# A hybrid decoder trunk: the recurrence, its group norm and the self-attention in one block, with small side work at other places of the recurrence

## The reference

```python
proj = h @ w_in[l]
p_r, p_m, p_g = jnp.split(proj, [RWKV_IN, RWKV_IN + MLA_IN], axis=-1)
# RWKV: w_pre = w0 + tanh(wd) @ w_up ; a = sigmoid(a0 + ad @ a_up) ; then, token by token,
state = state * w_t + (state @ a_t) * b_t + v_t * k_t        # 8 heads of 64x64
y = (y - mean) * rsqrt(var + GN_EPS) * ln_g + ln_b           # group norm of each head
y = (y + sum(r * k * r_k) * v) * (sigmoid(gd) @ g_up)
# MLA: q = rms_norm(c_q) @ w_uq, kv = rms_norm(c_kv) @ w_ukv, rope, rms_norm of q and k, causal attention
# gMLP: u * (tril(ws) @ rms_norm(gelu(v)) + b)
```

## Time and profile before

| | us |
|---|---|
| median of 3 runs | 1892.87 (1888.97 to 1893.78) |
| profiled execution, its own time | 1892.21 |
| its span | 1890.5 |
| PE busy | 1764.2 (93%) |
| DVE busy | 613.0 (32%) |
| ACT busy | 387.6 (21%) |
| recurrence block, layer 0 (201.8 to 256.8) | 55.0 |
| attention block, layer 0 (257.3 to 324.8) | 67.5 |

### The profile page before, as it was taken

How to read it: one execution, slowest core, us unless ns; L and a number is a source line. 1 busy time by engine, 2 the same in 40 slices (tenths; PEclk the granted TensorE clock), 3 DMA queues, 4 the chain that set the end, 5 groups by cost and what they waited for, 6 DMA issues and landing times. The chain is left out here.

```text
span 1890.5 us, 26335 instructions
## 1 busy us (share of the span) xinstructions
PE 1764.2 (93%) x11146; PEld 869.5 (46%) x11146; DVE 613.0 (32%) x1163; ACT 387.6 (21%) x745; POOL 182.0 (10%) x223
## 2 busy tenths in 40 slices
PE   8989989999999999998699998999999999999986
PEld 6435755455444443433353467544554444343322
DVE  7247545136311111110233584522461111111102
ACT  3131254054000000000212313522530000000001
POOL 3000101004000000000300000000040000000001
PEclk9999999999999999999899999999999999999997
DMA  9502204234999999999840220153179999999996
GB/s 378 206 1 34 36 10 172 95 134 163 406 429 426 428 427 428 428 427 427 317 198 0 34 35 4 54 222 134 62 284 412 427 427 427 427 429 427 428 428 238
DMA packets 90489, 494.83 MB, mean 262 GB/s; under 512 B 45646, under 2 KB 50510, under 8 KB 62736
## 3 DMA queue, kind: packets, MB, share of 16 engines
q1 hardware_dynamic: 82672, 475.45, 61.6%
q0 software_dynamic: 7632, 17.74, 2.6%
q10 hardware_dynamic: 80, 0.13, 0.0%
HBM read 465.34 MB, written 36.18 MB: 265 GB/s over the span
## 5 line engine op out<-in xcount | busy, mean ns | idle before, releaser
L2175 PE MATMUL bank<-ring,hT 128*64 128x512 f32 x2048 | 465.8, 597 | 37.6 <-DMA ring<-in_we 31.2
L2175 PEld LDWEIGHTS bank<-ring,hT 128*64 128x64 f32 x2048 | 139.6, 137 | 313.3 <-issue 251.0
L1059 PE MATMUL bank<-hT,ring 128*128 128x512 f32 (+1 forms) x576 | 249.9, 593 | 0.0
L2183 PE MATMUL bank<-ring,arena 128*64 128x512 f32 x1040 | 236.7, 597 | 11.4 <-DMA ring<-in_we 9.4
L1059 PEld LDWEIGHTS bank<-hT,ring 128*128 128x128 f32 (+1 forms) x576 | 107.9, 188 | 138.5 <-issue 137.2
L2160 PE MATMUL bank<-shift_in,arena 128*128 128x256 bf16 (+1 forms) x1440 | 160.0, 268 | 0.0
L2160 PEld LDWEIGHTS bank<-shift_in,arena 128*128 128x128 bf16 x1440 | 129.9, 98 | 62.6 <-issue 48.7
L2228 DVE TENSOR_TENSOR hT<-bank,colp 128x512 f32<-128x512 f32 (+1 forms) x68 | 45.3, 668 | 340.0 <-PE bank L2160 328.5
L2564 ACT ACTIVATE arena<-bank 128x256 f32<-128x256 f32 x65 | 24.9, 383 | 605.0 <-PE bank L2146 605.0
L2193 POOL DMA_INDIRECT expert_rows<-arena,row_places x63 | 62.1, 985 | 847.2 <-DVE arena L2705 818.6
L2183 PEld LDWEIGHTS bank<-ring,arena 128*64 128x64 f32 x1040 | 71.0, 136 | 144.0 <-issue 126.5
(11 more groups left out here) (464 smaller groups left out, 1885.6 us busy)
## 6 DMA issues: line engine op xcount, KB each, us to landing
ring<-in_we SPq DMA_DIRECT2D x193, 2048.0 KB, 22.9
ring<-in_w_in SPq DMA_DIRECT2D x6, 2048.0 KB, 19.2
expert_rows<-ring SPq DMA_DIRECT2D x1, 8448.0 KB, 25.8
ring<-in_w_out SPq DMA_DIRECT2D x4, 2048.0 KB, 9.5
ring<-in_wm SPq DMA_DIRECT2D x2, 2048.0 KB, 7.5
ring<-in_w_in SPq DMA_DIRECT2D x2, 1920.0 KB, 16.7
ring<-in_w_in SPq DMA_DIRECT2D x2, 1664.0 KB, 26.9
ring<-in_w_in SPq DMA_DIRECT2D x2, 1152.0 KB, 28.5
```

The source lines that it names most:

```text
L1059: last = nc.tensor.matmul(B[n % 4][0:w, :], ins_units[unit][:, k, u0:u0 + w], hT[:, k, :], start=k == 0, stop=k == KD - 1)
L2175: last = nc.tensor.matmul(bank[CAP * j:CAP * j + CAP, :], x[:, k, :], ahead_w[4 * j + k] if third else up_w(u, j, k), start=k == 0, stop=k ...
L2183: last = nc.tensor.matmul(bank[CAP * half:CAP * half + CAP, :], hid[u][:, m, :], down_w(slot, m, half), start=m == 0, stop=m == HM - 1)
```

## The change

Four things are done.

- **One block.** The streams of recurrence and attention become functions (`recurrent_pe`, `attention_pe` and so on) that one `nc.Block()` calls one after the other on each engine. The block's end and `end_stage()` between them go. Attention's instructions wait for semaphores of the recurrence instead (`s_yc`, `s_o`, `s_tr`, `s_lv`). The projection's semaphores are cleared by SP at the start of `attention_sp`.
- **Side work moved.** The table below has the places. `latent_means` goes from `fill_last(4)` to `fill_last(0)`, before `products(5, 5)`, and `flip(vT, 2, 7)` behind that.
- **Order at attention's start.** `up_q(0)` goes ahead of the centring, `up_q(1)` ahead of `heads_summed`, `gate(0)` ahead of `spread(0)`. SP's loads of `wsm` and `gbb` wait for the last flip of the recurrence only.
- **Low-rank products.** `lora_a` and `lora_decay` become `lora_pair(0)` and `lora_pair(1)`: each makes two products of either kind, in turn.

| side work | before | after |
|---|---|---|
| GELU of `gv` (ACT) | after `flipped("b", 3)` | after `diagonal(0)` |
| GELU of `uT` (ACT) | after `u_kept(6)` | after `ak_v_kept(0)` |
| squares of `gv` (ACT) | before `u_kept(6)` | before `ak_v_kept(1)` |
| both roots (ACT) | before `out_kept(3)` | before `u_kept(5)` |
| copy of the means (DVE) | before `state_kept(5)` | before `state_kept(0)` |
| transpose of the means (PE) | `fill_first(6)` | `fill_first(3)` |
| columns copied (DVE) | before `state_kept(6)` | before `state_kept(3)` |
| sums of `gv` (DVE) | after `w_added(7)` | before `state_kept(3)` |
| gains of `t14`, `cq2` (DVE) | before `state_kept(3)` | before `state_kept(4)` |
| RoPE products (DVE) | before `state_kept(4)` | before `state_kept(5)` |
| both reciprocals (DVE) | block's end | before `state_kept(5)` |
| scaling of `gv` (DVE) | block's end | before `state_kept(6)` |

The diff, without lines that only change their indentation:

```diff
+            def recurrent_pe(eng):
...
+                def latent_means(b):
+                    for i in range(NT):
+                        t, rows = slice(i * P, (i + 1) * P), slice(32 * i, 32 * i + 32)
+                        nc.tensor.matmul(B[b][rows, 0:P], lat_pick[:, 0, :], sq14[:, t], start=True, stop=False)
...
+                    last.then_inc(s_lp, 1)
...
                         elif q == 3:
+                            eng.wait_ge(s_gm, 16)
+                            nc.tensor.transpose(B[6][:, 0:P], lat_rows, ident[:, :]).then_inc(s_lp, 1)
                             eng.wait_ge(s_tc, FLIPS["k", 2])
                             flip(vT, 3, 7)
...
                             products(4, 5)
                             eng.wait_ge(s_wbc, 2)
-                            flip(vT, 2, 7)
+                            eng.wait_ge(s_la, SQUARES)
+                            latent_means(7)
                             eng.wait_ge(s_gm, 10)
                             products(5, 5)
+                            eng.wait_ge(s_lv, MEANS_KEPT)
+                            flip(vT, 2, 7)
...
-            end_stage()
...
+            def attention_sp(eng):
+                clear(late)
+                eng.wait_ge(s_tr, FLIPS["k", 3])
                     eng.dma_start(wsm, wsT_d[lay].rearrange("a p g n -> p (a g) n")).then_inc(s_gw, 16)
...
+            def attention_pool(eng):
+                eng.wait_ge(s_o, NC)
                     eng.memset(gn_rs, 0.0).then_inc(s_gz, 1)
...
+                eng.wait_ge(s_lv, SCALED)
+                up_q(0)
+                eng.wait_ge(s_yc, NC // 2)
                     for c in range(RC):
                         nc.tensor.matmul(B[c][:, :], head_centre[:, :], rT[:, c, :], start=True,
                                          stop=True).then_inc(s_gn1, 1)
-                    up_q(0)
+                up_q(1)
                     eng.wait_ge(s_gn3, RC)
                     heads_summed(B[4], gn_sq).then_inc(s_gn4, 1)
-                    up_q(1)
                     up_q(2)
-                    eng.wait_ge(s_gn5, 1)
-                    spread(0)
                     eng.wait_ge(s_gn2, RC)
                     gate(0)
+                eng.wait_ge(s_gn5, 1)
+                spread(0)
                     up_q(3)
+                eng.wait_ge(s_lv, KEYS_SCALED)
                     up_k(0)
...
-                    for c in range(RC):
-                        eng.wait_ge(s_ap, c + 1)
-                        eng.activation(X4[:, c, :], B[4 + c][:, :], ACT.Tanh, scale=0.5,
...
+                    for z in range(2):
+                        for n in range(2):
+                            c = 2 * z + n
+                            eng.wait_ge(s_ap, c + 1)
+                            eng.activation(X4[:, c, :], B[4 + 2 * n][:, :], ACT.Tanh, scale=0.5,
...
+            with nc.Block() as block:
...
+                @block.tensor
+                def _(eng):
+                    recurrent_pe(eng)
+                    attention_pe(eng)
...
+            release_late()
             leave_stage()
```

More of the change, by code:

```diff
@@ L238, in build @@
         s_e = [layer_sem(f"expert_weights{u}") for u in range(6)]
+        s_li = [layer_sem(f"inverse_start_loaded{z}") for z in range(2)]
         ring_flat = ring[:, :, :].rearrange("p u n -> p (u n)")
@@ L1169, in w_state, with products @@
+            def recurrent_pe(eng):
+                def products(q, b):
+                    tok = tokens_of(q)
+                    for cc in range(2):
+                        for m, (lt, rt) in enumerate(((kT, AT), (BT, rT), (kT, rT))):
+                            o = (3 * cc + m) * C
                             for e in range(2):
@@ L1180, in u_rows @@
                         for h in range(4):
+                            o = 256 * z + C * h
                             for R in HALVES:
[L1182 to L1194 removed]
@@ new lines, in u_rows, with state @@
+                def u_rows(q):
+                    eng.wait_ge(s_wbc, q // 2 + 1)
+                    if q:
+                        eng.wait_ge(s_wc, q)
+                    for h in range(4):
+                        for R in HALVES:
+                            last = nc.tensor.matmul(B[0][R, h * C:(h + 1) * C], XU[R, 4 * q + h, :],
+                                                    Wm[R, q % 4, h * C:(h + 1) * C], start=True, stop=True)
+                    last.then_inc(s_u, 1)
+                def state(q, left, right, first):
+                    for cc in range(2):
+                        for g, R in enumerate(HALVES):
+                            for e in range(2):
+                                hs = slice((2 * cc + e) * C, (2 * cc + e + 1) * C)
+                                last = nc.tensor.matmul(B[1 + g][64 * e:64 * e + 64, cc * C:(cc + 1) * C],
+                                                        left[R, q, hs], right[R, hs], start=first and cc == 0,
+                                                        stop=not first and cc == 1)
+                    return last
@@ new lines, in out_state @@
+                def out_state(q):
+                    for cc in range(2):
+                        for g in range(2):
+                            for e in range(2):
+                                rows, o = slice(64 * e, 64 * e + 64), P * cc + C * (q % 2)
+                                nc.tensor.matmul(B[3 + g][rows, o:o + C], ST[q % 2][rows, cc + 2 * g, :],
+                                                 rT[rows, cc + 2 * g, tokens_of(q)],
+                                                 start=q % 2 == 0 and cc == 0, stop=False)
@@ new lines, in out_local @@
+                def out_local(q, m, Z):
+                    for cc in range(2):
+                        for g, R in enumerate(HALVES):
+                            for e in range(2):
+                                rows, o, h = slice(64 * e, 64 * e + 64), P * cc + C * (q % 2), 2 * cc + e
+                                last = nc.tensor.matmul(B[3 + g][rows, o:o + C], Z[R, h * C:(h + 1) * C],
+                                                        big[R, q, h, m, :], start=q == 0 and m == 2 and cc == 0,
+                                                        stop=q % 2 == 1 and m == 1 and cc == 1)
+                    return last
```

1277 lines of the change are left out of this document (618 added, 659 removed).

## The result

The changed kernel takes 1871.15 us (median of six runs, 1867.19 to 1874.66) where the kernel before took 1892.13 us (six runs on the same chip, 1888.97 to 1897.55). The ratio is 0.9885, with a 95% interval from 0.9864 to 0.9906. That is 21 us less; I had forecast 12 us less, 1880.5 us, and a range that ended at 1876. The direction was right, and the size lies outside what I allowed for. The profiled execution of the changed kernel took 1873.28 us, its span is 1871.5 us, 19.0 us shorter than the 1890.5 us of before.

A forecast was written before the change was run, and what follows sets the result against it. The prediction took the experts to start when attention ends, so time saved in recurrence or attention shortens the span. Seams -10.67 and recurrence -1.3, summed as -12.0 from 1892.2, gave 1880.2, forecast as 1880.5 us; range 1876 to 1887.

The forecast's parts named there:

- The step that failed: Low-rank products in the projection: as many as before, four decay products in 3.70 us, so zero, or 0.3 either way.
- The seam: Recurrence's last product to the queries' first flip: 20.89 us, gaining 4.95 in layer 0 and 5.72 in layer 1.
- The wait for the queries: TensorE's wait before the first flip of the queries in attention: to grow from 0.83 to about 1.4 us.
- ScalarE as the late one: Barrier after the recurrence: ScalarE's table load and late output copy, and VectorE's scaling of `gv`, named as unneeded side work.
- The recurrence: Moved means products give 0.5 and `w_state(5)` starting earlier is part of the count; net -0.65 us per layer, -1.3 in all.
- no moved operation held TensorE for a microsecond: Sign: the prediction is wrong if a moved operation has TensorE waiting inside a recurrence chunk for over 1 us.
- The experts: From the end of attention on, both profiles have the same lengths, stretch by stretch; the experts only start earlier.
- The clock: At the seam: without the idle gap full clock holds in the centring; otherwise the gain is some 1.8 us less per layer.
- "better" rival: Recurrence of layer 1: its half-clock stretch vanishes, 1.07 us and about as much at its start, giving 1877; chance 0.06.

The follow-up runs named there:

- pair_alone: The kernel before with only the a and decay low-rank products alternating in pairs, barrier and side work as before: 1885.11 us, ratio 0.9965.
- same_half: The changed kernel with each pair's second product reading operand rows 64:128 like the first, so the output is wrong: 1878.99 us, ratio 0.993.
- busy_seam: The kernel before with four unused 128x512 products added on TensorE behind the recurrence's last one, in the gap at the barrier: 1885.73 us, ratio 0.9967.
- before_again: The kernel before, unchanged, profiled a second time: 1894.05 us in one run.
- no_pair: The changed kernel with low-rank products and tanhs in the old order, four a products behind tile 5, four decay products behind tile 6: 1881.59 us, ratio 0.9942.
- same_rows_first: The changed kernel with the two a products of each group ahead of its two decay products, waits and banks kept: 1872.68 us, ratio 0.989.

## Why the prediction was wrong, point by point

- **The step that failed** is the last one of the part on the recurrence: "The low-rank products are as many as before; TensorE goes through all four decay products in 3.70 without waiting, and the tanhs end with the same product. Zero, or 0.3 either way." I counted the products and looked for waits, and did not ask whether two of them can run at once. They can, on different halves of the operand rows: 1.92 us for four instead of 3.63, 6.8 us in four groups. `pair_alone` (6.7 us less) and `same_half` (7.7 us more) show this step by itself. With 6.8 us more the sum would have been 18.8, and the forecast 1873.7, within the runs of the changed kernel. No case among my rivals had it, so the range could not hold it either.
- **The seam** was right in its mechanism and nearly in its size. Forecast 20.89 us from the last product to the first flip, measured 20.32 and 20.33. In layer 0 the terms are: up to the spread 10.56 (forecast 10.67), to VectorE's first operation behind it 1.23 (1.24), VectorE until the queries' RoPE 2.28 (2.60), and from there to the flip 6.25 (6.38). The wait for the queries grew from 0.83 to 1.15, not to 1.4. The gain is 5.5 and 6.3 us, 11.8 in all, against 10.67.
- **What the seam's gain is made of** I had left open. It takes the experiments to see that its parts don't add. In layer 0, with the barrier kept, the moved side work and the new order behind the barrier give 25.84 - 21.35 = 4.5 us (mostly 2.9 us of gap, and 1.8 us of clock that the gap had cost), and the barrier the last 1.0. Without the barrier, the roots and `gv` cost only 0.37. That suggests that either edit alone finds most of the gain, since both remove the same wait; it is not shown, as no run drops the barrier with all of the side work and the order left as they were.
- **ScalarE as the late one.** I said that ScalarE's table load and copy were late for the barrier, and that VectorE scales `gv`. Both rows were right, but I listed them side by side. They are one chain: the copy ended at 255.02, and the `gv` product, which waited for the roots behind the table load, ended last, at 256.38, and set the gap.
- **The recurrence**: from its first to its last product it took 51.80 us on average in the eight layers profiled with the old side work, and 50.91 in the eighteen with the new, 0.9 us less per layer against a forecast of 0.65. Within this lie differences of up to 3.4 us from layer to layer with the same instructions (49.87 and 53.24 with the old side work), so the size is hardly known. `w_state(5)` followed `out_local(4)` at once (240.16 behind 239.66), and no moved operation held TensorE for a microsecond; in layer 0 its longest wait for another engine inside the loop is 0.61 us, for VectorE in chunk 6, where it had been 0.23.
- **The experts**: +0.2 us in each layer; "same lengths behind attention" held there. It did not hold from the first flip to the end of attention in layer 1, 47.4 instead of 45.7 us, by the clock.
- **The clock** at the seam went as the prediction had it, and `busy_seam` shows the cause. The Trainium skill, "TensorE: Matmul & The Clock Gate", Part 1, says that idleness puts TensorE at half clock; for the idle barrier the traces agree, with 5.37 us behind the gap and 3.67 us with the gap filled. My "better" rival built on a stretch of half clock in the recurrence of layer 1, which `before_again` does not have: it does not belong to the program. Its number did not follow from its own terms either; twice 1.07 us off the forecast is about 1878, not 1877.

In sum: 6.8 for the pairing, 11.8 for the seams, 1.8 for the recurrence are 20.4 us off 1892.2, which is 1871.8; the median is 1871.15. So close a match is luck, as the third term is known to a microsecond or two at best. What the profiles show beside that goes both ways: the flips at half clock in 7 of 18 layers, and in the changed kernel's own profile the slow sums of layer 0 and the fast spread of layer 1.

Two things stay open. Nobody knows from these runs why the clock falls at the flips in some executions and not in others, with the same 1.15 us of idleness before them. And `no_pair` lost 3 us more than its products account for. The intervals allow that; in its trace the part beside the projections is 2.2 us in the recurrences, 52.08 and 51.87 us against 51.46 and 50.29, at a granted clock of 1.00 in both kernels. Why recurrences of the same instructions differ in length is open.

## What to carry to other kernels

Where a change reorders products, look at which operand rows each one uses: here two products of 64 rows in different halves cost the time of one (0.96 us a pair), so "as many as before" is no price. At a barrier ask which engine ends last, which chain it waited in, and whether the next stage needs that work; removing the barrier or moving the work may be worth nearly the same, and not twice. And a wait of TensorE in a stretch that it bounds is worth more than its length when its clock falls behind it: here filling one in each layer with unused products gave 5.5 us, and filling two others in each layer with the next tile gave 12.

## What the runs showed of the hardware that I had not expected

- Products on different halves of the operand rows need not start in the order of the program: in `same_rows_first` a product on rows 0:64 started 0.02 us behind one on rows 64:128, and so ahead of another of the latter that stands before it in the program.
- Half clock costs a layer 1.7 us at the flips in some executions and nothing in others, in one program: 1.95 us or up to 3.28 us for the same sixteen flips, both behind a wait of 1.15 us.
- Unused products made a kernel faster (0.9967): with them the granted clock stayed at 1.00 through a barrier, and the centring took 3.67 us instead of 5.37.
